# A decoder layer with product-key experts: the bf16 high half of the gated activations moves from VectorE to ScalarE, and U blocks are loaded one place earlier on SyncE's queue

## The chip, the cores and the metric

The kernel runs on one core of a Trainium2 chip. The metric is device time in microseconds (us), the median of several runs. Engines are named as the profile names them: PE (TensorE, matrix products; PEld is its weight load), DVE (VectorE), ACT (ScalarE), POOL (GpSimd) and SP (SyncE, which here only issues DMA transfers). A "q" behind a name (SPq) is the engine's sequencer, the part that waits for semaphores and issues DMAs.

## The reference

One decoder layer over 1024 tokens of width 1024: two kinds of attention, a layer norm, then PEER, a layer of 16384 single-neuron experts of which each token uses 16 per head, and a second layer norm. The change touches only the expert part:

```
u = expert_u[idx]
h = gelu(einsum('thkd,td->thk', u, xb), approximate=False)
w = (g * h).astype(xb.dtype)
return einsum('thk,thkd->td', w, expert_v[idx])
```

Here `idx` are the chosen experts and `g` their softmax weights. Inputs and results are float32.

## The kernel before

The kernel has three phases: attention, routing (query products, top-k, a table of gates in device memory) and the expert phase, in which all of the change lies. The expert phase treats the tokens in two ways at once.

Five of the eight tiles of 128 tokens are computed **densely**: every one of the 16384 experts is evaluated for all 640 tokens, and the gate, zero for the experts that were not chosen, picks out the result. The experts come in 128 blocks of 128. For a block b, `up` multiplies the U block with the tokens (`h_psum`), ACT applies Gelu into `act_out` (L1595), DVE multiplies by the gate (L1665), and `down` multiplies with the V block into `o_psum`. Because PE works on bf16 and the data are float32, every operand is split into a bf16 high half (a copy to bf16) and a bf16 low half (value minus high half), and three of the four products are summed. So for each block there are three splits: U (`u_split`: high half on ACT L1587, low half on DVE L1677), V (`v_split`: ACT L1604, DVE L1688) and the gated activations (`w_split`: high half on DVE L1667, low half on DVE L1669).

The other three tiles are **gathered**: POOL fetches, for each of their 128 tokens, the rows of U (first half of the phase) or V (second half) of the experts chosen, 512 KB at a time, by indirect DMA into a ring of six buffers (L1641). DVE consumes each fetch in one instruction, here called a pick (L1702 for U, L1706 for V). There are 6 picks for each block on average.

The blocks go in groups of four, 32 groups in all. PE's order in a group is: up, down of tile 0, up, down of tile 1, up, down of tile 2, up, down of tile 3, down of tile 4 (`up_and_down`). The downs of a group run while the ups of the next group are made. DVE's work for one block is called a **step** in this document, and its four steps in a group are steps 0 to 3. A step is `gate_and_split`, then the low half of U for block b+2, then the low half of V for block b, then picks and the addition of one finished `o_psum` tile into the accumulator (L1694). By the table `DOWN_TILES`, steps 0 to 2 have one addition and 4, 5 and 5 picks; step 3 has two additions and 10 picks. `o_psum` is double-buffered, so the down of a tile waits until DVE has added the tile two places before it.

ACT's order for a block is: Gelu of b, high half of V of b, high half of U of b+2 (`blocks_of`). SP's order is in `refill`: wait until U's split of block b is done, load U of b+2; wait until V's split of block b is done, load V of b+2; after every fourth block wait for `w_done` and load the gates of a later group (L1552, 1280 KB). The raw U and V blocks have two buffers each. All of these transfers are on SP's queue and are issued in that order; the fetches are on POOL's queue.

## Time and profile before

| | |
|---|---|
| median of 3 runs | 3163.55 us (3163.04 to 3173.81) |
| the profiled execution's own time | 3160.89 us |
| its span, first to last instruction | 3159.1 us |
| PE busy | 2749.3 us, 87% |
| DVE busy | 2502.0 us, 79% |
| ACT busy | 770.7 us, 24% |
| POOL busy | 1137.8 us, 36% |
| mean granted PE clock | 0.925 |

The busy shares are means over phases with different limits. The expert phase is the last 1.9 ms of the span, and there PE, DVE and the DMA engines are all nearly full, so what bounds it has to be read from single groups: where each engine sits idle, and what ended that idle time. The granted clock is given as a fraction of full speed (1.0 is 2.4 GHz, 0.5 is 1.2 GHz).

### The profile page before, as it was taken

Reading aid. Unit: us, or ns where it says so; the run is one execution under the profiler, and the core shown is the slowest. Engines: PE = TensorE matmul, PEld = TensorE weight load, DVE = VectorE, ACT = ScalarE, POOL = GpSimd, SP = SyncE. Lnnn points to the kernel's source line nnn. Section 1 sums busy time; section 2 is a strip of 40 time slices with the busy share of each in tenths; the row PEclk is TensorE's granted clock in tenths of the full one; section 3 lists DMA queues with packets and bytes.
Section 4 is the critical chain, followed back from the end, with each engine's and each line's share of the span. In section 5 each row is a group of like instructions: output and inputs, shape, how many; then the busy total and the mean of one; then the engine's idle time right before and its main releaser. Section 6 shows DMA issues by size and latency. Waiting matters only on the chain. (4 is left out here: it accounts for less than half of the span.)

```text
span 3159.1 us, 47167 instructions
## 1 busy us (share of the span) xinstructions
PE 2749.3 (87%) x17293; PEld 1762.0 (56%) x17459; DVE 2502.0 (79%) x4669; ACT 770.7 (24%) x1295; POOL 1137.8 (36%) x841
## 2 busy tenths in 40 slices
PE   8999999798967745599999999989999899999995
PEld 3666655458966644355555555555555555555552
DVE  3344545366999998589889898988989998989998
ACT  2333323211124446112121121211212112112120
POOL 2110000110010000355555555555555555555554
PEclk9999988799978865799999999999999999999998
DMA  3000020260002243899989999989899898999993
GB/s 144 21 14 15 14 74 14 100 234 21 2 27 107 107 167 164 312 329 321 315 316 321 323 324 329 321 299 334 307 316 317 313 321 304 314 313 317 327 315 142
DMA packets 262961, 685.26 MB, mean 217 GB/s; under 512 B 35625, under 2 KB 118185, under 8 KB 258353
## 3 DMA queue, kind: packets, MB, share of 16 engines
q0 software_dynamic: 110592, 402.70, 35.6%
q1 hardware_dynamic: 152240, 280.98, 25.5%
q8 instruction: 64, 1.05, 0.1%
q14 instruction: 65, 0.52, 0.1%
HBM read 624.89 MB, written 58.72 MB: 216 GB/s over the span
## 5 line engine op out<-in xcount | busy, mean ns | idle before, releaser
L1831 PE MATMUL o_psum<-v_split,w_split 128*128 128x512 bf16 x3713 | 866.1, 391 | 123.6 <-DVE wide L1694 111.8
L1813 PE MATMUL h_psum<-early 128*128 128x384 bf16 (+1 forms) x6144 | 860.5, 300 | 51.0 <-DVE early L1677 26.0
L1813 PEld LDWEIGHTS h_psum<-early 128*128 128x128 bf16 x6144 | 602.0, 98 | 310.6 <-issue 61.0
L1831 PEld LDWEIGHTS o_psum<-v_split,w_split 128*128 128x128 bf16 x3840 | 382.5, 100 | 587.4 <-DVE wide L1694 123.9
L1641 POOL DMA_INDIRECT early<-u_rows,pick_index x320 | 419.8, 1312 | 444.7 <-DVE dots L1702 324.4
L1641 POOL DMA_INDIRECT early<-v_blocks,pick_index x320 | 423.0, 1322 | 380.4 <-DVE wide L1706 308.3
L1706 DVE SCALAR_TENSOR_TENSOR wide<-early,dots,wide 128x1024 f32<-128x1024 f32 x320 | 400.0, 1280 | 61.2 <-DMA early<-v_blocks,pick_index 59.3
L1702 DVE CUSTOM_DVE_ANT_0 early<-early,wide 128x1024 f32<-128x1024 f32 x320 | 382.1, 1220 | 68.9 <-DMA early<-u_rows,pick_index 65.7
L1587 ACT ACTIVATE early<-early 128x1024 bf16<-128x1024 f32 x128 | 135.2, 1057 | 1101.2 <-DMA early<-u_blocks 1090.6
L1100 PE MATMUL r_t_psum<-rt_x_t,early 128*128 128x128 f32 (+1 forms) x1920 | 237.5, 286 | 0.0
L1100 PEld LDWEIGHTS r_t_psum<-rt_x_t,early 128*128 128x128 f32 x1920 | 232.3, 202 | 0.0
L1130 PE MATMUL g_psum<-rt_hot 128*128 128x128 bf16 x1280 | 119.3, 263 | 127.8 <-DVE rt_hot L1435 127.5
L1694 DVE SCALAR_TENSOR_TENSOR wide<-wide,o_psum 128x1024 f32<-128x1024 f32 x160 | 194.3, 1214 | 0.0
L1201 ACT ACTIVATE wide<-g_psum 128x512 f32<-128x512 f32 x160 | 157.2, 1087 | 150.4 <-PE g_psum L1130 150.4
L1595 ACT ACTIVATE act_out<-h_psum 128x384 f32<-128x384 f32 (+1 forms) x256 | 96.8, 430 | 372.5 <-PE h_psum L1813 364.9
L1677 DVE TENSOR_TENSOR early<-early 128x1024 bf16<-128x1024 f32 x128 | 155.9, 1219 | 35.3 <-ACT early L1587 22.1
L1130 PEld LDWEIGHTS g_psum<-rt_hot 128*128 128x128 bf16 x1280 | 102.6, 119 | 143.5 <-DVE rt_hot L1435 70.8
L1688 DVE TENSOR_TENSOR v_split<-early,v_split 128x1024 bf16<-128x1024 f32 x128 | 155.9, 1218 | 0.0
L1604 ACT ACTIVATE v_split<-early 128x1024 bf16<-128x1024 f32 x128 | 135.4, 1058 | 0.0
L559 DVE TENSOR_SCALAR att_o_rows<-a_o_psum,att_row_sum 128x64 f32<-128x64 f32 x64 | 18.2, 284 | 130.3 <-PE a_o_psum L348 129.8
L1665 DVE TENSOR_TENSOR act_out<-act_out,gate 128x640 f32<-128x640 f32 x128 | 105.9, 827 | 13.0 <-ACT act_out L1595 8.6
L1669 DVE TENSOR_TENSOR w_split<-act_out,w_split 128x640 bf16<-128x640 f32 x128 | 105.7, 826 | 4.4
(200 smaller groups left out, 3014.7 us busy)
## 6 DMA issues: line engine op xcount, KB each, us to landing
early<-u_blocks SPq DMA_DIRECT2D x128, 512.0 KB
early<-v_blocks SPq DMA_DIRECT2D x128, 512.0 KB
gates<-wide SPq DMA_DIRECT2D x20, 2048.0 KB, 6.4
gate<-gates SPq DMA_DIRECT2D x32, 1280.0 KB
early<-w_query SPq DMA_DIRECT2D x8, 1024.0 KB, 5.8
att_w_raw<-w_fox SPq DMA_DIRECT2D x4, 1536.0 KB, 7.0
early<-u_rows,pick_index POOLq DMA_INDIRECT x320
early<-v_blocks,pick_index POOLq DMA_INDIRECT x320
```

Source lines behind the costliest of these rows:

```text
L1100: mm = pe.matmul(t_psum[n % 2][:, j * P:(j + 1) * P], w_q[:, unit, c], x1_t[:, c, bass.ds(tile_of(t) * P, P)], start=(c == 0), stop=(c == ...
L1130: mm = pe.matmul(g_psum[four % 2][:, j % 4], hot[:, m % HOTS, 1, j // 2, :, j % 2], hot[:, m % HOTS, 2 + part, j // 2, :, j % 2], start=(p ...
L1201: act.activation(stage[:, k, :, token:token + 4].rearrange("p h t -> p t h"), g_psum[four][:, :, :], ACT.Copy).then_inc(g_copied, 1)
L1604: act.activation(v_split[:, p, q, 0], v_raw[:, j % 2], ACT.Copy).then_inc(v_hi_done, 1)
L1641: pool.indirect_dma_start(fetched[n % RING], None, source, bass.IndirectOffsetOnAxis(ap=pick_index[:, n % GATHERED, at:at + 1], axis=0)).t ...
L1677: dve.tensor_tensor(u_split[:, k, 1], u_raw[:, k].rearrange("p (c n) -> p c n", c=KD), u_split[:, k, 0], ALU.subtract).then_inc(u_lo_done, 1)
L1688: dve.tensor_tensor(v_split[:, p, q, 1], v_raw[:, q % 2], v_split[:, p, q, 0], ALU.subtract).then_inc(v_split_done, 1)
L1694: dve.scalar_tensor_tensor(row, row, scale, o_psum[(DENSE * p + t) % 2][:, :], ALU.mult, ALU.add).then_inc(o_added, 1)
L1702: dve.tensor_tensor_reduce(fetched[n % RING], fetched[n % RING], acc[:, tile], 1.0, 0.0, ALU.mult, ALU.add, dots[:, k, tile:tile + 1]).the ...
L1706: dve.scalar_tensor_tensor(acc[:, tile], fetched[n % RING], dots[:, k, tile:tile + 1], acc[:, tile], ALU.mult, ALU.add).then_inc(row_used, 1)
L1813: mm = pe.matmul(h_psum[k][:, half, 0:width * P], u_split[:, k, part, c], xs[:, first:first + width, xpart, c, :], start=(c == 0 and part ...
L1831: mm = pe.matmul(o_psum[(DENSE * p + t) % 2][:, half * 512:half * 512 + 512], w_split[:, p, q, part, t * P:(t + 1) * P], v_split[:, p, q, ...
```

## The change

There are two edits.

The high half of the gated activations is made by ACT (`split_w_hi`), behind the high half of U in ACT's order and ahead of the next block's Gelu. DVE keeps the product with the gate (`gate_block`) and the low half (`split_w_lo`), and the low half now stands behind the step's first picks, just ahead of its addition, instead of right behind the product.

SP loads a U block as soon as the U split of the block before it in the same buffer is done: in iteration b it loads U of b+4 ahead of the wait for V's split of b; before, it loaded U of b+2 there. Two loads ahead of the loop make up the difference.

```diff
                     for j in range(2 * GROUP):
                         b = 2 * GROUP * i + j
+                        if not (end and j >= 2 * GROUP - 4):
+                            sp.wait_ge(u_hi_done, b + 3)
+                            sp.wait_ge(u_lo_done, b + 3)
+                            load_u(b + 4, j % 2)
                         if not (end and j >= 2 * GROUP - 2):
-                            sp.wait_ge(u_hi_done, b + 1)
-                            sp.wait_ge(u_lo_done, b + 1)
-                            load_u(b + 2, j % 2)
                             sp.wait_ge(v_split_done, b + 1)
                             load_v(b + 2, j % 2)
...
+                def split_w_hi(b, j):
+                    act.wait_ge(gated, b + 1)
+                    act.activation(w_split[:, j // GROUP, j % GROUP, 0], act_out[:, j % 2], ACT.Copy
+                                   ).then_inc(w_hi_done, 1)
...
                             split_u_hi(b + 2, j % 2, GROUP * i + j // 2 + 2)
+                        split_w_hi(b, j)
...
                     dve.tensor_tensor(rows, rows, gate[:, p, :, q, :], ALU.mult).then_inc(gated, 1)
-                    dve.wait_ge(gated, b + 1)
-                    dve.tensor_copy(w_split[:, p, q, 0], act_out[:, k]).then_inc(w_hi_done, 1)
+
+                def split_w_lo(b, p, q):
                     dve.wait_ge(w_hi_done, b + 1)
-                    dve.tensor_tensor(w_split[:, p, q, 1], act_out[:, k], w_split[:, p, q, 0], ALU.subtract
+                    dve.tensor_tensor(w_split[:, p, q, 1], act_out[:, q % 2], w_split[:, p, q, 0], ALU.subtract
                                       ).then_inc(w_done, 1)
...
                                 take(i, kind, half * p + r)
+                            if t == DOWN_TILES[q][0]:
+                                split_w_lo(GROUP * g + q, p, q)
```

DVE's instructions of step 1 in the loop over the first half of the phase, before (L1665 is the product, L1667 and L1669 the high and low half of the activations, L1677 and L1688 the low halves of U and V, L1702 a pick, L1694 the addition):

```order
L1665 TENSOR_TENSOR act_out<-act_out,gate 128x640 [waits gelu_done]
L1667 CAST w_split<-act_out 128x640 [waits gated]
L1669 TENSOR_TENSOR w_split<-act_out,w_split 128x640 [waits w_hi_done]
L1674 REGISTER_ALU [waits u_in1]
L1677 TENSOR_TENSOR early<-early 128x1024 [waits h_done,u_hi_done]
L1688 TENSOR_TENSOR v_split<-early,v_split 128x1024 [waits v_hi_done,v_in1]
L1702 ISA early,dots<-early,wide 128x1024 [waits fetched_in4]
L1702 ISA dots 128x1
L1702 ISA fetched,dots<-fetched,wide 128x1024 [waits fetched_in5]
```

The same step after the change, where the lines are L1676 (product), L1688 and L1699 (U and V), L1713 (pick), L1680 (low half of the activations) and L1705 (addition):

```order
L1676 TENSOR_TENSOR act_out<-act_out,gate 128x640 [waits gelu_done]
L1685 REGISTER_ALU [waits u_in1]
L1688 TENSOR_TENSOR early<-early 128x1024 [waits h_done,u_hi_done]
L1699 TENSOR_TENSOR v_split<-early,v_split 128x1024 [waits v_hi_done,v_in1]
L1713 ISA early,dots<-early,wide 128x1024 [waits fetched_in4]
L1713 ISA dots 128x1
L1713 ISA fetched,dots<-fetched,wide 128x1024 [waits fetched_in5]
L1713 ISA dots 128x1
L1711 ISA
L1713 ISA early,dots<-early,wide 128x1024 [waits fetched_in0]
L1713 ISA dots 128x1
L1680 TENSOR_TENSOR w_split<-act_out,w_split 128x640 [waits w_hi_done]
```

The cast is gone, nothing that the next instruction needs stands right behind the product any more, and the low half has moved behind three picks (two in steps 0 and 3).

ACT's instructions for two blocks at the start of its loop, after the change (L1600 Gelu, L1609 high half of V, L1592 of U, L1613 of the gated activations; before, the rows are the same without L1613):

```order
L1600 ACTIVATE act_out<-h_psum 128x384 [waits w_done]
L1600 ACTIVATE act_out<-h_psum 128x256
L1609 ACTIVATE v_split<-early 128x1024 [waits o_done]
L1592 ACTIVATE early<-early 128x1024 [waits h_done,u_in0]
L1613 ACTIVATE w_split<-act_out 128x640 [waits gated]
L1596 REGISTER_ALU
L1600 ACTIVATE act_out<-h_psum 128x384 [waits w_done,h_done]
```

The next block's Gelu now stands behind an instruction that waits for DVE's product.

## Rows read from the trace of the kernel before

**Rows 1.** Windows: expert phase, groups, part of steps 1, 3; clock, DMA share last.

```profile
core 0: us, PE busy (x) PEld busy (x) DVE busy (x) ACT busy (x) POOL busy (x), PEclk, DMA share, GB/s
1295.76:3092.02 1796.26, 1667.16 (x9672) 965.13 (x9795) 1624.92 (x1950) 345.28 (x509) 988.77 (x756) 0.97 0.90 317
1920.13:1976.32 56.19, 55.12 (x326) 32.18 (x330) 50.98 (x76) 10.95 (x16) 32.71 (x25) 1.00 0.92 325
2722.76:2779.67 56.91, 51.91 (x301) 30.00 (x304) 51.86 (x50) 9.35 (x15) 31.43 (x25) 0.97 0.91 317
1930.23:1941.48 11.25, 11.20 (x70) 6.74 (x70) 11.18 (x17) 2.77 (x4) 6.66 (x5) 1.00 0.86 301
1952.73:1962.73 10.00, 9.95 (x65) 6.27 (x65) 9.93 (x15) 0.20 (x2) 5.81 (x4) 1.00 0.83 275
1962.73:1976.32 13.59, 13.54 (x81) 7.92 (x81) 8.65 (x16) 1.55 (x3) 8.60 (x7) 1.00 1.05 382
1966.00:1976.00 10.00, 9.95 (x65) 6.28 (x65) 6.17 (x10) 0.00 (x0) 5.71 (x6) 1.00 1.04 397
```

**Rows 2.** Waits in 1295.76:3092.02: us in total, times, longest.

```profile
ACT early L1587 <- DMA early<-u_blocks: 1090.6, 125, 20.4
PE o_psum L1831 <- DVE wide L1694: 92.8, 31, 5.5
DVE early L1702 <- DMA early<-u_rows,pick_index: 65.7, 33, 5.4
DVE wide L1706 <- DMA early<-v_blocks,pick_index: 59.3, 25, 5.9
DVE early L1677 <- ACT early L1587: 22.1, 6, 6.0
```

**Rows 3.** Timeline of step 1: start, length, instruction, idle before it and its releaser.

```profile
1926.21 6.68 PE L1813 MATMUL h_psum<-early 128*128 128x384 bf16 x48
...
1930.23 0.82 DVE L1665 TENSOR_TENSOR act_out<-act_out,gate 128x640 f32<-128x640 f32 x1
...
1931.08 0.49 DVE L1667 CAST w_split<-act_out 128x640 bf16<-128x640 f32 x1
1931.61 0.83 DVE L1669 TENSOR_TENSOR w_split<-act_out,w_split 128x640 bf16<-128x640 f32 x1
...
1932.35 1.22 DVE L1677 TENSOR_TENSOR early<-early 128x1024 bf16<-128x1024 f32 x1
...
1932.95 5.13 PE L1831 MATMUL o_psum<-v_split,w_split 128*128 128x512 bf16 x23
...
1934.62 1.22 DVE L1702 CUSTOM_DVE_ANT_0 early<-early,wide 128x1024 f32<-128x1024 f32 x1
```

**Rows 4.** Timeline of step 3 of the same group.

```profile
1952.73 0.82 DVE L1665 TENSOR_TENSOR act_out<-act_out,gate 128x640 f32<-128x640 f32 x1
...
1957.23 0.33 SPq L1478 DMA_DIRECT2D early<-v_blocks  x1
1957.78 0.56 SPq L1552 DMA_DIRECT2D gate<-gates  x1
...
1959.04 5.01 SPq L1478 DMA_DIRECT2D early<-u_blocks  x1
1959.12 1.17 POOL L1641 DMA_INDIRECT early<-u_rows,pick_index  x1 [3.38 <-DVE dots L1702]
...
1962.51 5.13 PE L1831 MATMUL o_psum<-v_split,w_split 128*128 128x512 bf16 x23
...
1968.62 1.23 DVE L1702 CUSTOM_DVE_ANT_0 early<-early,wide 128x1024 f32<-128x1024 f32 x1 [3.41 <-DMA early<-u_rows,pick_index]
```

**Rows 5.** Waits of SP's sequencer in 1295:3092.

```profile
SPq L1478 <- DVE v_split L1688: 1458.2, 126, 19.0
```

**Rows 6.** ACT's groups by shape in 1390:3110: busy us, mean ns.

```profile
L1604 ACT ACTIVATE v_split<-early 128x1024 bf16<-128x1024 f32 x120 | 126.9, 1058 | 0.0
...
L1595 ACT ACTIVATE act_out<-h_psum 128x384 f32<-128x384 f32 x120 | 58.0, 483 | 353.5 <-PE h_psum L1813 345.8 <-DVE w_split L1669 5.6 <-issue 1.8
```

More of the change, by code:

```diff
@@ L1571, in refill @@
                             load_gate(2 * i + 2 + j // GROUP, j // GROUP)
+                for b in range(2):
+                    sp.wait_ge(u_hi_done, b + 1)
+                    sp.wait_ge(u_lo_done, b + 1)
+                    load_u(b + 2, b)
                 with sp.Fori(0, last) as i:
@@ L1655, in _, with gate_block @@
                 dve.memset(eps[:, :], LN_EPS).then_inc(eps_set, 1)
-                def gate_and_split(b, g, p, q, n):
+                def gate_block(b, g, p, q, n):
                     k = q % 2
@@ L1727, in step @@
                     for q in range(GROUP):
-                        gate_and_split(GROUP * g + q, g, p, q, n)
+                        gate_block(GROUP * g + q, g, p, q, n)
                         split_u_lo(i, GROUP * g + q + 2, GROUP * p + q)
```

## The prediction

> **What bounds the kernel now.** Only the expert phase is touched, so I read that first, with the table of windows over the stretch from the first product with a gate to the last, and then over single groups of four blocks. In the 1796.26 us of the phase PE is busy 1667, DVE 1625 and the DMA share is 0.90 [rows 1]. The distance between the two ends is 127 steps, or 31.75 groups, so a group takes 56.6 us on average. The reader is to see that no engine is far from full, and that a busy share alone doesn't say which one sets the pace.
>
> The waits do. PE's largest wait is for DVE's additions: 92.8 us in 31 waits, one in each group [rows 2]. ACT waits 1090.6 us for U blocks, but ACT is busy only 345 us of the phase, and what it delays is small: DVE waits for ACT's high half of U in 6 places, 22.1 us together [rows 2]. DVE itself waits only for fetches, 65.7 + 59.3 us [rows 2]. So PE waits for DVE, and DVE either works or waits for a fetch: DVE with its fetches is the chain.
>
> Where in a group? In step 1 DVE is busy 11.18 of 11.25 us while the DMA share is 0.86 at 301 GB/s [rows 1]: the step is DVE's own work, and the transfers have room. In the steady group I read, DVE is busy 50.98 of 56.19 us [rows 1]; the idle 5.2 us lie in step 3, whose seventh pick waits 3.41 us for its fetch [rows 4]. In the first 10 us of step 3 the DMA share is 0.83 at 275 GB/s, and in ten later ones 1.04 at 397 [rows 1]. So steps 0 to 2 are bound by DVE, and the second part of step 3 by transfers.
>
> A comparison that the trace makes by itself: the group in the second half of the phase, with the same bytes, has 0.88 us more of DVE work (51.86 against 50.98) and is 0.72 longer (56.91 against 56.19) [rows 1]. A microsecond of DVE's work is worth nearly a microsecond.
>
> **Edit 1, the high half on ACT.** In step 1 the starts are: product 1930.23, cast 1931.08, low half 1931.61, low half of U 1932.35 [rows 3]. So the three cost 0.85 + 0.53 + 0.74 = 2.12 us. The low half, 0.83 us long and followed by an instruction that doesn't need it, costs 0.74; the product, 0.82 long, is now followed by such an instruction too, and I give it the same 0.74. After the change the two cost 1.48, so a step loses 0.64. If the product keeps its 0.85, the step still loses 0.53. Steps 0 to 2 are 96 of the 128: 96 x 0.64 = 61 us, at least 96 x 0.53 = 51.
>
> What hides the work that is moved: ACT's copy of 640 columns. The trace doesn't show it; it shows 1058 ns for 1024 columns and 483 ns for 384 [rows 6], which bound it, and on the line between them 640 columns come to 0.71 us. I take that. DVE asks for the result only after the low halves of U and V (1932.35 to 1934.62, 2.27 us) and two or three picks of 1.22 [rows 3], which is 4.7 us or more after the product. ACT is then not held by something else: its copy of U for b+2 stands ahead, and that block is now in place a step earlier. So the copy costs nothing; without its cover it would cost 0.71 on every step.
>
> The Trainium skill speaks against this move: in "ScalarE: Activation LUTs", Rules for kernel authors, simple elementwise work belongs on VectorE, which is there the faster engine per element. The rows agree that DVE is faster here (0.49 us for the cast against 0.71 estimated on ACT), and by the rule with the copy on the path the change would lose 0.18 us a step instead of gaining 0.53. It is not on the path as the rows stand.
>
> What waits behind the new wait: ACT's Gelu of b+1 is queued behind the copy, so it can't start before the product of b has ended, some 1.5 us into the step. PE's next use of that buffer is a whole block later, so nothing asks for it sooner. And the low half comes later: at 0.74 + 2.27 + 2.4 = 5.4 us into the step, done at 6.2, against 2.2 before. PE's first down of a group needs the fourth block's low half; it starts at 1962.51, which is 9.8 us after the start of step 3 at 1952.73 [rows 4]. The margin of 3.6 us covers a PE that runs up to that much further ahead. SP's load of gates, behind the same wait, is issued at about +6.2 instead of +5.05; it is for a later group.
>
> **Edit 2, U one place earlier.** SP's waits are nearly all for V's split, 1458.2 us in 126 [rows 5]: the U load, whose own condition was long met, stood behind it. In step 3 the loads were issued at +4.5 (V), +5.05 (gates) and +6.3 (U), and U's issue itself took 5.01 us behind the gates [rows 4]. After the change U goes out when its own low half is done, at 0.74 + 1.14 = +1.9, V at about +3.0, gates at +6.2. The same bytes move, but U and V fill the first ten microseconds of step 3, where the DMA engines have room, and U no longer competes with the fetches behind the gates. A U block is 0.52 MB, 1.3 us at the 397 GB/s of the later stretch [rows 1]. That is the most by which the last fetch of the step can come earlier from this. The seventh pick's fetch (issued at 1959.12, +6.4) is used at 1968.62, and in front of it are V and the gates; after the change also U. So the seventh pick hardly moves against the step's start and only what follows it is quicker. I take 0.8 us a group, 32 x 0.8 = 26 us. Bounds: below, the seventh pick comes a U block later, -1.3 a group; above, all of DVE's waiting goes until PE is the limit. PE's work in a group is 4 x 6.68 + 5 x 5.13 = 52.4 us [rows 3, 4], so a group can gain 56.6 - 52.4 = 4.2 at most, of which 1.9 is in steps 0 to 2, and 2.3 is left for step 3.
>
> The DMA page of the Trainium skill ("DMA: Bandwidth & Descriptors", Bandwidth) puts the limit between device memory and one core at about 358 GB/s. The row shows 397 over ten microseconds, so the trace doesn't agree for this one core. By the page's figure step 3, which moves 10 us x 275 GB/s and then 13.6 us x 382 GB/s [rows 1], some 7.9 MB, could not go under 22 us, an estimate that would leave 1.5 us of gain there.
>
> The six waits for U's high half (22.1 us) should mostly go, since U is there a step earlier; the first, 6.0, follows the first loads of the phase and stays. Of the other 16 I take 12.
>
> Against this I set 10 us, 0.3 a group, for places where PE and DVE, now both near their own limits, hold each other up.
>
> **The sum.** 61 + 26 + 12 - 10 = 89 us. The profiled execution took 3160.9, so 3071.9; the median of the runs lies 2.7 above the profiled one, which gives 3074. The parts of the span before and behind the phase don't change.
>
> **Rivals.**
> 1. Step 3 gives nothing: the last fetch lands at the same distance from the step's start, because the same bytes pass in it. For it: the gates' transfer still stands in front of the seventh fetch. Against it: the room in the first ten microseconds. The sum without the 26: 3100.
> 2. PE becomes the bound: the fetches no longer hold DVE, and a group takes PE's 52.4 plus 0.5 for joints. (56.6 - 52.9) x 32 = 118: 3045. For it: PE has only 92.8 us of that wait, and its granted clock is 0.97 over the phase, a mean of stretches at 2.4 GHz and a few at 1.2, against 1.00 in the steady group [rows 1]; some of that would come back. Against it: step 3's transfers.
> 3. Transfers take it all back: share 0.90 in the phase already, so DVE's saved time turns into waiting for fetches. 3160. Against it: the comparison of the two halves of the phase, and 0.86 in step 1.
> 4. Slower: in step 3 U, V and gates (0.52 + 0.52 + 1.31 = 2.36 MB) stand together on SP's queue in front of the seventh fetch, and hold all fetches behind it. At the 275 GB/s of that stretch they take 8.6 us. If the seventh pick is used later than now by more than the 1.9 us that steps 0 to 2 save, the group gets longer; with 2.7 later it is 0.8 x 32 = 26 us slower, 3189. It decides itself at +17.8 us into step 3, against +15.9 now. Against it: fetches and SP's loads are on different queues and share the engines, and the gates are issued later than now.
>
> **Chances.** The forecast 0.45 (its own range 3055 to 3092), rival 1 0.22, rival 2 0.19, rival 3 0.07, rival 4 0.07. Range for 8 in 10: from 3038, near rival 2's PE limit, to 3116, which takes in rival 1 with the lower price of 0.53 a step. About 0.5%, 16 us, is what a measurement can tell from no change. Faster 0.87, same 0.06, slower 0.07.
>
> **What would show it.** Steps 1 and 2 at 10.6 us instead of 11.25, with DVE still full in them; step 3 near 22.5 instead of 23.6 with the seventh pick's wait still there; the U load issued 1.9 us into a step and ACT's wait for it nearly gone, ACT waiting for the product instead; the low half never waiting for ACT's copy, about 0.7 us; PE's wait for the additions down from 3 us a group to about 1. I am wrong if step 3 grows by as much as the others shrink (transfers), if the low half waits for ACT, or if PE waits for `w_done` at the first down of a group.

## The result and the profile after

| | before | after |
|---|---|---|
| median | 3166.12 us (3163.04 to 3173.81, 4 runs) | 3024.33 us (3020.01 to 3029.14, 4 runs) |
| profiled execution, span | 3160.89, 3159.1 | 3029.14, 3027.3 |
| expert phase, first to last product | 1796.26 us | 1664.88 us |
| sum of steps 0 / 1 / 2 / 3 over the groups | 353.0 / 363.8 / 362.2 / 717.3 | 318.9 / 351.7 / 343.8 / 650.4 |

The kernel is faster: the ratio is 0.9554, interval 0.9539 to 0.957. I had forecast 3074 with a range of 3038 to 3116, so the direction was right and the size wrong: the gain is 142 us, not 89, and the time lies below the range. The 128 products have 127 distances between them: 32 each for steps 0 to 2, and 31 for step 3. The step sums in the last line are worked out from their start times in the trace. Steps 0 to 2 gave 64.6 us together and step 3 gave 66.9. All of the gain lies in the expert phase (131.4 of the 131.8 us between the two profiled executions). The other 10 us of the 142 are spread between executions: the median lies 5 us above the profiled execution before, and 5 below it after.

The windows of the kernel after: the phase, one group, its step 1, and its step 3 in two parts, to be read against [rows 1]. The group read takes 53.88 us by DVE's products, longer than the mean of 52.4 (1664.88 / 31.75), and its step 3 takes 22.8 us against a mean of 21.0.

```profile
core 0: us, PE busy (x) PEld busy (x) DVE busy (x) ACT busy (x) POOL busy (x), PEclk, DMA share, GB/s
1295.27:2960.15 1664.88, 1629.12 (x9662) 957.76 (x9785) 1555.72 (x1822) 427.38 (x636) 1118.71 (x756) 0.99 0.95 342
1868.68:1922.56 53.88, 53.67 (x323) 31.79 (x326) 48.93 (x72) 13.34 (x20) 33.80 (x26) 1.00 0.97 352
1878.13:1888.73 10.60, 10.55 (x67) 6.54 (x67) 10.60 (x16) 2.29 (x5) 7.18 (x5) 1.00 1.02 398
1899.79:1909.79 10.00, 10.00 (x49) 4.70 (x48) 8.99 (x14) 2.42 (x3) 5.62 (x4) 1.00 0.84 284
1909.79:1922.56 12.77, 12.72 (x81) 7.82 (x80) 9.20 (x16) 2.65 (x4) 8.54 (x8) 1.00 1.03 368
```

DVE's work in the phase fell by 69.2 us (1624.92 to 1555.72), which is the 128 casts and little else. The phase fell by 131.4, so DVE's idle time fell by the other 62.2. PE is now idle for 35.8 us of the phase, against 129.1 before, and the same bytes pass at 342 GB/s instead of 317. PE is also busy for 38.0 us less (1667.16 to 1629.12) with the same products. Before, the granted clock stood at its lower level, 1.2 GHz, for 92.2 us of the phase in 19 stretches; after, for 20.5 us in 5. At half the clock half of a stretch is lost, which makes 35.9 us of the difference. Before, 13 of the 19 stretches begin within 1.3 us of the end of a stand of PE of 3.0 to 4.9 us, as in this row, where the 24 products take 7.04 us instead of 5.34, with a granted clock of 0.53 from 2351.00 to 2354.40:

```profile
2350.39 7.04 PE L1831 MATMUL o_psum<-v_split,w_split 128*128 128x512 bf16 x24 [4.49 <-DVE wide L1694]
```

In step 1 DVE has no idle time, and the step takes 10.60 us instead of 11.25.

The waits of the kernel after in the phase that answer to those of [rows 2], and ACT's new one:

```profile
ACT w_split L1613 <- DVE act_out L1676: 540.8, 103, 18.3
...
DVE wide L1717 <- DMA early<-v_blocks,pick_index: 38.6, 53, 2.4
DVE early L1713 <- DMA early<-u_rows,pick_index: 32.6, 34, 2.7
...
PE o_psum L1844 <- DVE wide L1705: 15.2, 12, 4.2
DVE early L1688 <- ACT early L1592: 13.8, 10, 8.3
...
ACT early L1592 <- DMA early<-u_blocks: 7.1, 1, 7.1
```

Four things are to be read there. PE's wait for the additions fell from 92.8 us in 31 waits to 15.2 in 12. DVE's waits for fetches fell in these two rows from 125.0 us to 71.2, and the longest from 5.9 to 2.7. ACT's wait for U blocks (1090.6 us) is gone but for the first. And ACT's largest wait, for the product, has no one behind it: the list has no wait of DVE's low half for ACT's copy at all. One of the prediction's signs of being wrong, PE waiting for `w_done`, shows once, 5.9 us at PE's first down, and not in the groups behind it.

The same group's step 1, of which [rows 3] has the one before (product, low half of U, ACT's copy, low half of V, the two loads, the late low half, the addition, the next product):

```profile
1878.13 0.82 DVE L1676 TENSOR_TENSOR act_out<-act_out,gate 128x640 f32<-128x640 f32 x1
1878.87 1.22 DVE L1688 TENSOR_TENSOR early<-early 128x1024 bf16<-128x1024 f32 x1
1878.98 0.74 ACT L1613 ACTIVATE w_split<-act_out 128x640 bf16<-128x640 f32 x1 [0.80 <-DVE act_out L1676]
...
1880.36 0.34 SPq L1478 DMA_DIRECT2D early<-u_blocks  x1
...
1884.58 0.82 DVE L1680 TENSOR_TENSOR w_split<-act_out,w_split 128x640 bf16<-128x640 f32 x1
...
1885.32 1.21 DVE L1705 SCALAR_TENSOR_TENSOR wide<-wide,o_psum 128x1024 f32<-128x1024 f32 x1
...
1888.73 0.82 DVE L1676 TENSOR_TENSOR act_out<-act_out,gate 128x640 f32<-128x640 f32 x1
...
1889.92 1.23 DVE L1688 TENSOR_TENSOR early<-early 128x1024 bf16<-128x1024 f32 x1 [0.36 <-ACT early L1592]
```

Product and low half take 0.74 us each from start to next start, as assumed; ACT's copy is done at 1879.72, and its reader starts 4.86 us later. The last row, in step 2, has a small new wait: ACT's high half of U comes 0.36 us late, behind the Gelu that PE's up released. In step 3 the same wait is 1.01 us. This is how PE's pace now reaches DVE.

Step 3 of that group, against [rows 4]: the loads, the seventh pick, and the waits behind it.

```profile
1899.79 0.82 DVE L1676 TENSOR_TENSOR act_out<-act_out,gate 128x640 f32<-128x640 f32 x1
...
1903.06 0.33 SPq L1478 DMA_DIRECT2D early<-u_blocks  x1
...
1907.19 0.56 SPq L1552 DMA_DIRECT2D gate<-gates  x1
...
1912.84 1.23 DVE L1713 CUSTOM_DVE_ANT_0 early<-early,wide 128x1024 f32<-128x1024 f32 x1
...
1915.61 1.23 DVE L1713 CUSTOM_DVE_ANT_0 early<-early,wide 128x1024 f32<-128x1024 f32 x1 [0.41 <-DMA early<-u_rows,pick_index]
...
1918.10 1.23 DVE L1713 CUSTOM_DVE_ANT_0 early<-early,wide 128x1024 f32<-128x1024 f32 x1 [1.25 <-DMA early<-u_rows,pick_index]
...
1920.27 1.23 DVE L1713 CUSTOM_DVE_ANT_0 fetched<-fetched,wide 128x1024 f32<-128x1024 f32 x1 [0.94 <-DMA fetched<-u_rows,pick_index]
```

The seventh pick starts 13.05 us into the step, where it started at 15.89 before, and the profile shows no wait for its fetch; before it waited 3.41. The waits at the three last picks have grown, from 0.67 us together to 2.60. The 31 steps 3 of each trace, taken together, say the same with other sizes, and show what each edit does to the pick:

| kernel | seventh pick starts at | it waits | the three last picks wait |
|---|---|---|---|
| before | +16.38 us | 3.65 us | 0.55 us |
| U ahead of the gates, one place | +15.76 | 2.99 | 0.51 |
| U early, alone (edit 2) | +15.06 | 2.34 | 0.43 |
| after | +13.13 | 0.33 | 1.57 |
| after, gates earlier | +14.48 | 0.94 | 0.28 |

(Means, worked out from the start times of DVE's picks; the kernels between before and after are those of the next section.) The pick moved by 3.25 us, 1.32 of them with edit 2 alone. The step became only 2.2 us shorter, because part of the wait came back behind the pick. My prediction had both parts wrong: the pick moves, and what follows it does not become quicker.

### The profile page after: what moved, and what is told of

It is laid out like the page before. It is cut to its first block, busy times and chain, and to the rows that moved or that the text cites. A ratio compares the mean times of both kernels' runs of the same rounds, so it can differ in the third digit from the quotient of the medians.

```text
span 3027.3 us, 47212 instructions
## 1 busy us (share of the span) xinstructions
PE 2715.5 (90%) x17293; PEld 1756.0 (58%) x17459; DVE 2432.0 (80%) x4541; ACT 853.5 (28%) x1423; POOL 1268.7 (42%) x841
## 4 chain that ended last, share of the span: by engine, by line
PE 23%; issue 12%; DMA 10%; DVE 9%; POOL 2%; SPq 1%; ACT 0%; DVEq 0%; POOLq 0%; ACTq 0%
PE h_psum L1826 12%; PE o_psum L1844 11%; DMA early<-v_blocks,pick_index 6%; DMA fetched<-v_blocks,pick_index 3%; DVE wide L1717 2%; POOL early L1652 2%; DVE early L1713 1%; DVE early L1688 1%; DVE v_split L1699 1%; DVE wide L1705 1%; DMA fetched<-u_rows,pick_index 1%; DVE act_out L1676 1%; SPq L1552 1%; POOL fetched L1652 1%; DVE w_split L1680 1%
## 5 line engine op out<-in xcount | busy, mean ns | idle before, releaser
L1844 PE MATMUL o_psum<-v_split,w_split 128*128 128x512 bf16 x3713 | 832.0, 382 | 46.2 <-DVE wide L1705 33.6
L1844 PEld LDWEIGHTS o_psum<-v_split,w_split 128*128 128x128 bf16 x3840 | 375.9, 98 | 482.5 <-DVE wide L1705 40.1
L1652 POOL DMA_INDIRECT early<-v_blocks,pick_index x320 | 491.4, 1536 | 229.0 <-DVE wide L1717 146.3
L1652 POOL DMA_INDIRECT early<-u_rows,pick_index x320 | 441.5, 1380 | 332.4 <-DVE dots L1713 212.0
L1713 DVE CUSTOM_DVE_ANT_0 early<-early,wide 128x1024 f32<-128x1024 f32 x320 | 382.6, 1220 | 34.5 <-DMA early<-u_rows,pick_index 32.6
L1613 ACT ACTIVATE w_split<-act_out 128x640 bf16<-128x640 f32 x128 | 94.3, 736 | 637.5 <-DVE act_out L1676 544.7
L1600 ACT ACTIVATE act_out<-h_psum 128x384 f32<-128x384 f32 (+1 forms) x256 | 97.4, 432 | 610.2 <-PE h_psum L1826 553.8
L1705 DVE SCALAR_TENSOR_TENSOR wide<-wide,o_psum 128x1024 f32<-128x1024 f32 x160 | 194.0, 1212 | 0.0
L1688 DVE TENSOR_TENSOR early<-early 128x1024 bf16<-128x1024 f32 x128 | 155.8, 1218 | 24.3 <-ACT early L1592 13.8
L1699 DVE TENSOR_TENSOR v_split<-early,v_split 128x1024 bf16<-128x1024 f32 x128 | 155.7, 1217 | 0.0
L1592 ACT ACTIVATE early<-early 128x1024 bf16<-128x1024 f32 x128 | 135.1, 1056 | 17.9 <-PEq L1070 10.8
L1609 ACT ACTIVATE v_split<-early 128x1024 bf16<-128x1024 f32 x128 | 135.4, 1058 | 1.4 <-DMA early<-v_blocks 1.4
L1676 DVE TENSOR_TENSOR act_out<-act_out,gate 128x640 f32<-128x640 f32 x128 | 105.0, 820 | 14.1 <-ACT act_out L1600 9.0
```

The source lines that it names most:

```text
L1609: act.activation(v_split[:, p, q, 0], v_raw[:, j % 2], ACT.Copy).then_inc(v_hi_done, 1)
L1652: pool.indirect_dma_start(fetched[n % RING], None, source, bass.IndirectOffsetOnAxis(ap=pick_index[:, n % GATHERED, at:at + 1], axis=0)).t ...
L1688: dve.tensor_tensor(u_split[:, k, 1], u_raw[:, k].rearrange("p (c n) -> p c n", c=KD), u_split[:, k, 0], ALU.subtract).then_inc(u_lo_done, 1)
L1699: dve.tensor_tensor(v_split[:, p, q, 1], v_raw[:, q % 2], v_split[:, p, q, 0], ALU.subtract).then_inc(v_split_done, 1)
L1705: dve.scalar_tensor_tensor(row, row, scale, o_psum[(DENSE * p + t) % 2][:, :], ALU.mult, ALU.add).then_inc(o_added, 1)
L1713: dve.tensor_tensor_reduce(fetched[n % RING], fetched[n % RING], acc[:, tile], 1.0, 0.0, ALU.mult, ALU.add, dots[:, k, tile:tile + 1]).the ...
```

## The experiments

Each was timed beside the kernel before on the same chip; those runs of before had medians from 3164.02 to 3170.45. "Phase" is the distance between first and last product of the profiled execution, and the steps are sums over the groups, worked out as above.

| kernel | median us | ratio (interval) | phase | steps 0 / 1 / 2 / 3 |
|---|---|---|---|---|
| before | 3166.12 | | 1796.3 | 353 / 364 / 362 / 717 |
| U early, alone (edit 2) | 3104.57 | 0.9812 (0.9779 to 0.9846) | 1735.0 | 338 / 363 / 362 / 672 |
| U ahead of the gates, one place | 3125.32 | 0.986 (0.9827 to 0.9892) | 1761.7 | 339 / 364 / 362 / 697 |
| ACT high half, alone (edit 1) | 3250.25 | 1.0266 (1.0228 to 1.0305) | 1882.9 | 495 / 345 / 356 / 686 |
| the same, gates earlier | 3179.4 | 1.0025 (0.9995 to 1.0056) | 1835.0 | 435 / 353 / 356 / 691 |
| the same, U ahead of the gates | 3092.92 | 0.9768 (0.9742 to 0.9794) | 1732.3 | 319 / 376 / 352 / 685 |
| after | 3024.33 | 0.9554 (0.9539 to 0.957) | 1664.9 | 319 / 352 / 344 / 650 |
| after, gates earlier | 3033.75 | 0.9588 (0.9556 to 0.9621) | 1664.5 | 319 / 354 / 344 / 648 |
| after, cast on DVE | 3076.87 | 0.9726 (0.9698 to 0.9753) | 1708.8 | 335 / 359 / 358 / 657 |
| after, low half at once | 3136.39 | 0.9894 (0.9869 to 0.9918) | 1776.3 | 348 / 371 / 370 / 688 |
| after, half picks | 2996.39 | 0.9457 (0.9435 to 0.9478) | 1635.8 | 261 / 366 / 359 / 650 |
| before, gates in step 1 | 3332.29 | 1.052 (1.0482 to 1.0559) | 1966.0 | 333 / 376 / 648 / 608 |
| U early, gates in step 1 | 3025.08 | 0.956 (0.9529 to 0.959) | 1662.3 | 334 / 363 / 367 / 599 |
| after, gates in step 1 | 3000.48 | 0.9472 (0.945 to 0.9494) | 1637.1 | 319 / 356 / 358 / 605 |

### The two edits apart

**U early, alone.** The kernel before with edit 2.

```diff
+                        if not (end and j >= 2 * GROUP - 4):
+                            sp.wait_ge(u_hi_done, b + 3)
+                            sp.wait_ge(u_lo_done, b + 3)
+                            load_u(b + 4, j % 2)
                         if not (end and j >= 2 * GROUP - 2):
-                            sp.wait_ge(u_hi_done, b + 1)
-                            sp.wait_ge(u_lo_done, b + 1)
-                            load_u(b + 2, j % 2)
                             sp.wait_ge(v_split_done, b + 1)
```

> The kernel before with edit 2 alone: SP issues U of b+4 ahead of the wait for V's split; the high half stays on DVE. Theory A (step 3 got shorter because U no longer stands behind the gates on SP's queue): step 3 falls from 23.2 us to about 21.5, the six waits for U's high half go, and the time is near 3166 - 32 x 1.7 - 16 = 3096. Theory B (it got shorter because the gates' transfer is issued behind the seventh pick's fetch instead of ahead of it): here the gates are still issued ahead of that fetch, so the seventh pick's wait stays 3 us or more, step 3 loses 0.5 at most, and the time is near 3166 - 16 - 16 = 3134.

**ACT high half, alone.** The kernel before with edit 1.

```diff
+                def split_w_hi(b, j):
+                    act.wait_ge(gated, b + 1)
+                    act.activation(w_split[:, j // GROUP, j % GROUP, 0], act_out[:, j % 2], ACT.Copy
+                                   ).then_inc(w_hi_done, 1)
...
-                    dve.wait_ge(gated, b + 1)
-                    dve.tensor_copy(w_split[:, p, q, 0], act_out[:, k]).then_inc(w_hi_done, 1)
...
+                            if t == DOWN_TILES[q][0]:
+                                split_w_lo(GROUP * g + q, p, q)
```

> The change with edit 1 alone: high half on ACT, low half behind the first picks, SP's order as before. The gates, which wait for the low half, are issued about 7 us into step 3, behind the seventh pick's fetch. Theory A (U's place made step 3 shorter): step 3 stays at 23, steps 0 to 2 lose 0.64 each, the waits for U stay: 3166 - 61 = 3105. Theory B (the gates' place): step 3 falls to about 21.2 us although U is issued late, and the time is near 3166 - 61 - 60 = 3045, U's hiccups keeping it above the change's 3024.

Edit 2 alone saves 61 us, 45 of them in step 3, where I had given it 26, and 15.5 in step 0. The first theory fits: step 3 takes 672.2 / 31 = 21.7 us where it gave 21.5, the time is 9 us above its 3096, and the seventh pick's wait is under the 3 us of the second theory. Edit 1 alone costs 85 us, which neither theory had (3105 and 3045). Together they save 142, so they are not a sum of two parts: the second makes the first possible. The loss is not in ACT or DVE's work (step 1 is down by 18 us). It is in step 0, whose sum rose from 353 to 495. This is the timeline around the joint of steps 3 and 0, in the kernel with edit 1 alone:

```profile
1933.98 0.56 SPq L1552 DMA_DIRECT2D gate<-gates  x1
...
1934.78 11.72 SPq L1478 DMA_DIRECT2D early<-u_blocks  x1
...
1948.40 0.82 DVE L1671 TENSOR_TENSOR act_out<-act_out,gate 128x640 f32<-128x640 f32 x1
...
1955.51 1.06 ACT L1587 ACTIVATE early<-early 128x1024 bf16<-128x1024 f32 x1 [15.00 <-DMA early<-u_blocks]
...
1956.60 1.22 DVE L1683 TENSOR_TENSOR early<-early 128x1024 bf16<-128x1024 f32 x1 [7.38 <-ACT early L1587]
```

The late low half holds back the gates on SP's queue (they wait for `w_done`), the issue of U behind them takes 11.72 us where the same issue behind a V block takes 0.33, U lands only after step 0 has begun, ACT's high half is late, and DVE stands for 7.38 us. The kernel before escapes it narrowly at the same place, here in the step 0 that follows [rows 4]:

```profile
1977.00 1.06 ACT L1587 ACTIVATE early<-early 128x1024 bf16<-128x1024 f32 x1 [12.72 <-DMA early<-u_blocks]
...
1978.45 1.22 DVE L1677 TENSOR_TENSOR early<-early 128x1024 bf16<-128x1024 f32 x1
```

ACT's copy ends at 1978.06 and DVE asks for it 0.39 us later. Edit 1 lets DVE ask 1.4 us earlier in the step. ACT's start also tells when the block had landed, since it waited for it: before, 16.4 us (median of 30, from 13.5 to 23.3) after the start of an issue right behind the gates, and 5.7 us (4.0 to 7.4) behind a V block. The block is 10.7 us late, although the gates' 1.31 MB are worth 3.3 us at 397 GB/s. Sometimes the kernel before waits as well: "DVE early L1677 <- ACT early L1587: 22.1, 6, 6.0" in [rows 2] is the same wait. With edit 1 alone it has grown to

```profile
DVE early L1683 <- ACT early L1587: 185.3, 51, 9.5
```

### Where U's early load pays

**U ahead of the gates, in one place of four.** The kernel before, with one load moved.

```diff
-                            sp.wait_ge(u_hi_done, b + 1)
-                            sp.wait_ge(u_lo_done, b + 1)
-                            load_u(b + 2, j % 2)
+                            if j % GROUP:
+                                sp.wait_ge(u_hi_done, b + 1)
+                                sp.wait_ge(u_lo_done, b + 1)
+                                load_u(b + 2, j % 2)
                             sp.wait_ge(v_split_done, b + 1)
                             load_v(b + 2, j % 2)
+                        if j % GROUP == GROUP - 1 and not (end and j == 2 * GROUP - 1):
+                            sp.wait_ge(u_hi_done, b + 2)
+                            sp.wait_ge(u_lo_done, b + 2)
+                            load_u(b + 3, (j + 1) % 2)
```

> The kernel before with one move: in the one place of four where a group's gates are fetched (step 3), the load of U is issued ahead of the gates instead of behind them. In the other steps U keeps its place behind the wait for V's split, and ACT's work is that of before. Theory 1: all that U's move (edit 2) gives in step 3 comes from this one place, where U's issue stood behind the gates' transfer. Then step 3 takes 21.0 to 21.8 us instead of 22.4, which is some 40 of edit 2's 61 us, and the time is 3115 to 3130 us. Theory 2: what counts is U's earlier start in every step, which takes it off the fetches that follow. Then this move gives little, step 3 stays above 22.2 us, and the time is 3145 to 3165 us.

The time, 3125.3, fell in the band of the first theory, but by its parts neither theory holds whole. The phase lost 34.5 us of the 61.3 that edit 2 gives: 14.5 of step 0's 15.5, and 20.6 of step 3's 45. A step 3 takes 696.7 / 31 = 22.5 us; the first theory wanted 21.0 to 21.8. So a good half of edit 2's gain is this one place. The rest goes with the other difference between the two kernels, U's earlier start in each step (3.6 us into it instead of 5.1). The step 3 read in each trace shows the same order: the seventh pick waited 3.41 us before [rows 4], and in this kernel and with edit 2 alone, one row each:

```profile
1951.65 1.22 DVE L1710 CUSTOM_DVE_ANT_0 early<-early,wide 128x1024 f32<-128x1024 f32 x1 [3.14 <-DMA early<-u_rows,pick_index]
```

```profile
1944.98 1.23 DVE L1707 CUSTOM_DVE_ANT_0 early<-early,wide 128x1024 f32<-128x1024 f32 x1 [1.97 <-DMA early<-u_rows,pick_index]
```

Why this last half is so large is not settled. The same bytes pass in the step, and a U block is 0.52 MB, 1.3 us; yet step 3 with edit 2 alone is 45 / 31 = 1.5 us shorter. What shrinks is DVE's idle time in step 3, by 44.7 us (142.0 to 97.3, over 31 steps). The trace doesn't say which DMA engine carried which packet, so I can't show whether one engine lagged behind the others.

**ACT high half with the gates earlier, and with U ahead of the gates.** Edit 1 alone, and in the one kernel the gates wait for the product instead of the low half,

```diff
                         if j % GROUP == GROUP - 1 and not end:
-                            sp.wait_ge(w_done, b + 1)
+                            sp.wait_ge(gated, b + 1)
```

while in the other U is moved ahead of the gates in one place, with the lines of the diff above.

> Edit 1 alone again, but the gates' load waits for the product instead of for the low half, so that it is issued about 3 us earlier in step 3 and U's load of the next step stands less far behind. Theory C (edit 1 alone is slower because the low half, now late, holds back the gates on SP's queue and U behind the gates, so that U comes after step 0 has asked for it): step 0 falls from 15.7 us to 10 to 11, DVE's 185 us of waits for ACT's high half of U shrink under 60, and the time is near 3110. Theory D (it is slower because ACT's copy for the activations stands in front of its other work): step 0 stays at 15 us and the time near 3250.

> Edit 1 alone, with SP's order as before except at one place in four: the U load that followed the gates on SP's queue is issued ahead of them; the other three stay behind V's split. Theory C (edit 1 alone was 85 us slower because U stood behind the gates' transfer while DVE asked for it 1.4 us earlier in the step and step 3 was shorter): step 0 falls from 15.7 us to about 10, and with steps 1 and 2 at 10.6 to 11 and step 3 near 21 the time is near 3040. If U's later place in the other three steps matters as well: steps 1 and 2 above 11.2, or DVE's waits for the high half of U above 40 us in all, and 3080 to 3120.

The gates' earlier issue brought 71 of the 85 us back. Step 0 still costs 435 us, or 13.6 a step, and the waits for ACT's high half are 136.8 us, so the result lies between theories C and D, and the delay of the gates is only a part of the cause. In the second kernel U's place took step 0 to 319, the value of the kernel after, and made a gain of 73 us of a loss of 85. So the loss of edit 1 is the place of U behind the gates, and the delay of the gates makes it longer. But this kernel still stands 69 us above the kernel after, in the band of the expectation's second case. Its steps 1 and 3 are longer (376 against 352, 685 against 650), and ACT's high half of U is late in 38 places, 57.1 us together:

```profile
ACT early L1595 <- DMA early<-u_blocks: 653.7, 101, 11.0
...
DVE early L1691 <- ACT early L1595: 57.1, 38, 8.4
```

A U block that is loaded just before it is needed has no reserve once steps are shorter. Edit 2's load runs one block further ahead in every step, and that is what the shorter steps need.

**After, gates earlier.** The kernel after with the same exchange of `w_done` for `gated`: the gates go out 3.7 us into step 3 instead of 6.4 (medians).

> The changed kernel with the gates' load waiting for the product (the last reader of the gates) instead of for the low half, so that it is issued right behind V's load, at about 3.5 us into step 3 and ahead of the seventh pick's fetch. Theory B: the seventh pick waits 2 to 3 us again, step 3 grows from 20.7 to about 22.5, and the time is near 3024 + 32 x 1.5 = 3072. Theory A: no change, 3024 within 8 us.

The length of step 3 did not change: 648 us against 650, in a phase of 1664.5 against 1664.9. The median is 9 us higher, just outside the 8 of theory A, but the intervals of the two ratios overlap. So the theory that step 3 became short because the gates now stand behind the seventh fetch falls. The place of the gates does decide which pick waits, though: with the gates earlier the seventh pick starts 1.35 us later and the three last picks wait 1.29 us less (the table of the last section). In the kernel after, moving the gates by 2.7 us moves the wait and does not remove it.

### Edit 1, taken apart

**After, cast on DVE.** The high half goes back to DVE, right behind the product; the low half stays late.

```diff
-                        split_w_hi(b, j)
...
                     dve.tensor_tensor(rows, rows, gate[:, p, :, q, :], ALU.mult).then_inc(gated, 1)
+                    dve.wait_ge(gated, b + 1)
+                    dve.tensor_copy(w_split[:, p, q, 0], act_out[:, k]).then_inc(w_hi_done, 1)
```

> The changed kernel with the high half back on DVE, right behind the product; the low half stays late and U early. It prices ACT's copy alone against the cast. If DVE bounds steps 0 to 2: each step is 0.63 us longer, and the time rises by what PE's limit of 51.8 us a group doesn't swallow: 3024 + 96 x 0.64 = 3085, to 3105 with step 3. It also shows whether the low half's late place, without the cast's move, does anything: if so the time differs by over 15 us from the 3104.6 of edit 2 alone.

**After, low half at once.** ACT makes the high half, and DVE's low half stands right behind the product again, so that ACT's copy is on DVE's path.

```diff
                         gate_block(GROUP * g + q, g, p, q, n)
+                        split_w_lo(GROUP * g + q, p, q)
                         split_u_lo(i, GROUP * g + q + 2, GROUP * p + q)
...
-                            if t == DOWN_TILES[q][0]:
-                                split_w_lo(GROUP * g + q, p, q)
```

> The changed kernel with the low half of the activations put back right behind the product, the high half still on ACT, so that ACT's 0.74 us copy lies on DVE's path in every step. If the cover of the first picks is what makes the copy free: each step costs some 0.75 to 0.9 us more, 1.0 where ACT is still at U's high half; in the half bound by DVE all of it shows, in the other part of it, so 3024 + 128 x 0.6 = 3100. If the cover is worth nothing (PE sets the time anyway): within 15 us of 3024.

From edit 2 alone (3104.6) to the cast on DVE with a late low half (3076.9) is 28 us, and from there to the kernel after (3024.3) is 53. So the two halves of edit 1 give 28 for the order and 53 for the engine, once U has its reserve; by the profiled phases it is 26 and 44. Of the 26, step 3 has 15.4, nearly all of it idle time of DVE (97.3 to 82.2 us). With the low half out of the way, DVE's first picks and SP's loads of U and V stand 0.9 us earlier in the step, and the gates 1.8 us later; which of these does it, no run shows. The time lies 8 us below the 3085 of the expectation.

With the copy on the path, the kernel is 112 us slower than after (3136.4, where I expected 3100), and also 32 us slower than edit 2 alone, which has the same order and the cast on DVE. The wait is there by name:

```profile
DVE w_split L1680 <- ACT w_split L1613: 102.2, 117, 9.2
```

That is 0.25 us a block (32 / 128) in the very comparison for which I had worked out 0.18. The Trainium skill's rule ("ScalarE: Activation LUTs", Rules for kernel authors: simple elementwise work goes to VectorE) holds here where the copy is waited for, and is turned round where 4.86 us of other work cover it.

### What limits the kernel now

**After, half picks.** Each pick works on 512 of its 1024 columns. This leaves out half of the sums of the gathered tiles, and all transfers stay.

```diff
-                        dve.tensor_tensor_reduce(fetched[n % RING], fetched[n % RING], acc[:, tile], 1.0, 0.0,
+                        dve.tensor_tensor_reduce(fetched[n % RING][:, 0:HALF], fetched[n % RING][:, 0:HALF],
+                                                 acc[:, tile, 0:HALF], 1.0, 0.0,
```

> The changed kernel with DVE's picks on the first 512 of the 1024 columns of each fetched row; all transfers stay. It leaves out half of the gathered dot products and sums. DVE loses about 0.53 us on each of 768 picks, 13 us in a group of 52. If PE is the bound of the changed kernel: PE's start-to-start 4 x 6.74 + 5 x 4.96 = 51.8 us a group remains and the time falls only from 3024 to about 3005. If DVE with its fetches still is the bound: it falls by 8 us a group or more, below 2800.

DVE's work in the phase falls by 392 us, and the time by 28. The starts of PE's ups (L1829) and downs (L1847) in a group show why:

```profile
1912.18 6.68 PE L1829 MATMUL h_psum<-early 128*128 128x384 bf16 x48
...
1918.70 5.34 PE L1847 MATMUL o_psum<-v_split,w_split 128*128 128x512 bf16 x24
...
1923.88 6.68 PE L1829 MATMUL h_psum<-early 128*128 128x384 bf16 x48
```

An up takes 6.52 us from start to next start and a down 5.18, so a group cannot be under 4 x 6.52 + 5 x 5.18 = 52.0 us at this clock. Taken from the start of every fourth up in each trace, 29 of 31 groups take 52.0 us in the kernel with half picks, all but the first two. In the kernel after it is 18 of 31, and in the kernel before none. So PE sets the pace of most groups of the kernel after; but for the first two, the others lie in the half that fetches V and take 52.4 to 58.1 us. The mean over the phase, 1635.8 / 31.75 = 51.5 us with half picks against 1664.9 / 31.75 = 52.4 in the kernel after, can lie under the floor of a full group because the first group's ups have no downs between them. The 28 us between the two kernels are what DVE with its fetches still costs.

**Gates in step 1.** The gates are loaded in step 1 instead of step 3, in three kernels: the one before, the one with edit 2 alone, and the one after.

```diff
-                        if j % GROUP == GROUP - 1 and not end:
-                            sp.wait_ge(w_done, b + 1)
-                            load_gate(2 * i + 2 + j // GROUP, j // GROUP)
+                        if j == 1:
+                            sp.wait_ge(w_done, b)
+                            load_gate(2 * i + 1, 1)
+                        if j == GROUP + 1 and not end:
+                            sp.wait_ge(w_done, b)
+                            load_gate(2 * i + 2, 0)
```

> The kernel before with one thing moved: the gates of a later group are loaded in step 1 of a group instead of step 3, one group later, so 1.31 MB leave step 3 and go where the DMA engines have room. Nothing else of the change is in it. Theory B (the gates' transfer ahead of the seventh fetch sets step 3): step 3 falls from 23.2 to about 20 us, bounded by DVE's own 18.2 there, steps 1 keep their 11.25, and the time is near 3166 - 32 x 2.7 = 3080. Theory A (U's place): step 3 stays above 22.5 and the time above 3140.

> Edit 2 alone with the gates in step 1, no edit 1. In the kernel before, the gates in step 1 cost 167 us. If that was U standing behind the gates with no step in hand, early U removes the cost: step 2 stays near 11.3 us, step 3 falls under 21 us as DVE's own 18.2 plus small waits allows, and the time is near 3104.6 - 31 x 1.5 = 3058. If V behind the gates was part of the cost, step 2 shows it, 12 us or more, and the time is above 3105.

> The changed kernel with the gates loaded in step 1 instead of step 3, the move that cost 167 us in the kernel before. If that cost came from U, which was needed within the step, it is gone here, since U now has a step in hand; V, which follows in the same queue and has no such reserve, could take its place. With U's reserve enough: step 3 shorter where DVE with its fetches is the bound, PE's 51.8 us a group the limit, 3005 to 3025. If V takes its place: step 2 grows by 5 us and more, 3150 or above.

The same move costs 167 us in the kernel before and gains 80 with edit 2 alone and 24 in the kernel after. No expectation had the 167 us (3080, or above 3140 with a long step 3), 3025 is 33 us better than the 3058 forecast for edit 2 alone, and 3000 is just under the range of 3005 to 3025 for the kernel after. It does what it is meant to do in all three: step 3 falls from 717 to 608, from 672 to 599 and from 650 to 605. But in the kernel before it puts U's issue behind the gates in step 1, and step 2 then stands for U: 648 us instead of 362. The trace of that kernel, and its wait:

```profile
1942.20 0.57 SPq L1552 DMA_DIRECT2D gate<-gates  x1
...
1943.01 7.25 SPq L1478 DMA_DIRECT2D early<-u_blocks  x1
...
1959.20 1.06 ACT L1589 ACTIVATE early<-early 128x1024 bf16<-128x1024 f32 x1 [15.77 <-DMA early<-u_blocks]
...
1960.29 1.22 DVE L1679 TENSOR_TENSOR early<-early 128x1024 bf16<-128x1024 f32 x1 [9.69 <-ACT early L1589]
```

```profile
DVE early L1679 <- ACT early L1589: 294.1, 40, 12.1
```

In the kernel after the slow issue is still there, and no one waits for it, because the block is for a step later:

```profile
1925.28 0.57 SPq L1552 DMA_DIRECT2D gate<-gates  x1
...
1934.90 3.33 SPq L1478 DMA_DIRECT2D early<-u_blocks  x1
```

The kernel after with its gates in step 1 is the fastest full version, 3000.48 us (2999.33 to 3002.37). PE's wait for the additions is one of 1.1 us there, and the phase is 1.4 us above that of the kernel with half picks: PE sets the pace, with 29 of 31 groups at 52.0 us. It also tells what edit 1 is worth when PE is nearly the bound: with U early and the gates in step 1, it adds 25 us (3025.1 to 3000.5), not 80.

```profile
PE o_psum L1846 <- DVE wide L1707: 1.1, 1, 1.1
```

## Why the prediction was wrong in size

**The step that failed: "the seventh pick hardly moves against the step's start and only what follows it is quicker. I take 0.8 us a group."** In the group read it moved from +15.89 to +13.05, in the mean from +16.38 to +13.13, and with edit 2 alone, which is what this step of the prediction was about, to +15.06. Step 3 lost 45.1 us with edit 2 alone, 1.5 us a group instead of 0.8. I had reckoned by bytes, the 1.3 us of one U block, in a step whose trace had a 5.01 us issue standing behind the gates [rows 4]. I wrote that row down and priced nothing from it. About half of the effect is that place (20.6 of 45 us); the other half goes with U's earlier start elsewhere, whose size I can't derive. Both edits together take 66.9 / 31 = 2.2 us from step 3, close to the 2.3 that I had named as the upper bound, but I had no reason for that size.

**The gap, term by term.** Against the profiled executions the gain is 131.8 us, and I had 89. Step 3 gave 19 more than forecast from edit 2 and 22 more from edit 1, no loss shows for which I had set 10 us aside ("hold each other up"), and steps 0 to 2 gave 8 less. The 10 us that are left to the 142 are the spread between executions.

**Edit 1 in step 3: taken as nothing, is 21.8 us.** I counted 96 steps because the second part of step 3 was bound by transfers. With edit 2 in place step 3 goes from 672.2 to 650.4 when edit 1 is added, 0.7 us a group: 13.9 us less of DVE's work and 7.9 less of its idle time. The fetches are themselves released by picks (POOL's issue at 1959.12 in [rows 4] waits for DVE's dots), so earlier picks also issue them earlier. That last reason is argued from the timeline; the kernel with the cast on DVE fits it, since it has 15.4 of the 21.8 us with the first picks 0.9 us earlier, but its loads of U and V go out earlier too.

**Edit 1 in steps 0 to 2: 61 us forecast, 48.4 measured.** With the waits for U I had 73, and the two edits together gave 64.6, but edit 2 alone has 16.2 of these, so edit 1 gave 48.4, under the 51 that I had called the least. The start-to-start times (0.74 and 0.74), the copy on ACT (0.71 estimated, measured below) and its cover held. DVE's own work in these steps fell by 54 us, 0.56 a step, and 6 us came back as new waits. Steps 1 and 2 of the group read are 10.60 and 11.06 us instead of 11.25. The second of them holds the new wait of 0.36 us. The copy's row:

```profile
L1613 ACT ACTIVATE w_split<-act_out 128x640 bf16<-128x640 f32 x128 | 94.3, 736 | 637.5 <-DVE act_out L1676 544.7
```

**The waits for U's high half: 12 of 16 us expected to go, 10.6 went.** With edit 2 alone all 16 went, and only the first, 5.9 us, stays. In the kernel after the first is 8.3 us of the 13.8; the other nine are 5.5, where five were 16.1. What I didn't see is that these six waits were the visible end of a mechanism: edit 1 alone makes 185.3 us of them. The prediction called that edit safe by itself ("ACT is then not held by something else: its copy of U for b+2 ... is now in place a step earlier") and leaned on edit 2 for it without asking what edit 1 does without. It was right about the pair.

**Rival 2, PE becomes the bound.** This is what happened in most groups; I gave it 0.19 and 3045 us. Its mechanism is shown three ways: 18 of 31 groups take the 52.0 us of PE's floor, PE's wait for the additions is 15.2 us, and half picks give only 28 us more. It missed its own time because I put the floor at 52.4 + 0.5. The 52.4 was added up from the lengths in the rows (6.68 and 5.13) and not from start to next start, which gives 52.0, and the 0.5 for joints does not show. The granted clock of the phase went from 0.97 to 0.99, as the rival said it would.

**Rival 1** (step 3 gives nothing) and **rival 3** (transfers take it back) are refuted: step 3 gave half of the phase's gain, and the rate of transfers rose from 317 to 342 GB/s with the demand. **Rival 4** (U, V and gates queue in front of the seventh fetch) is refuted by the seventh pick, which is at +13.13 in the mean, and at +14.48 even with the gates earlier, where the rival needed +17.8.

The limit of about 358 GB/s in the Trainium skill ("DMA: Bandwidth & Descriptors", Bandwidth) doesn't bind over a step here: step 1 moved 398 GB/s for 10.6 us. The same section says that with both cores of a memory domain streaming each gets about 358 GB/s, and it lists 425 GB/s for a 16 MB transfer on one core whose neighbour is idle, which is nearer to this kernel on one core and which I left out. Step 3 doesn't settle it. It takes 21.0 us on average (650.4 / 31) where the estimate from 358 GB/s gave 22, but in the group read it moved 7.5 MB (10.00 us at 284 GB/s and 12.77 at 368) and not 7.9, in 22.8 us.

## What to carry to other kernels

A load that stands behind a large transfer on one issuing queue is late by more than the bytes say (here 10.7 us behind 1.31 MB, which are worth 3.3 us at 397 GB/s): look in the timeline for an issue that takes microseconds instead of 0.33, and ask how many steps before its use the block was loaded. Two edits may each look like a separate saving and be worth -85 and +61 us alone and +142 together; before shortening a chain, give the loads that feed it a reserve. When PE waits 93 us for another engine and is busy for 93% of the stretch, work out PE's own floor from start-to-start times and give it a good chance of being the new end. A wait that has gone from one instruction may stand at the next ones: measure the whole step.

## What the runs showed of the hardware

The issue of a U block on SP's queue took 0.33 us behind a V block, and 4.20 to 12.87 us (median of 30: 5.29) right behind the gates' transfer of 1280 KB in the kernel before. From that issue to ACT's start on the block were 16.4 us (median) instead of 5.7. Issued in the next step instead, the block still took 3.02 us to issue (median) in the kernel after with the gates in step 1. The DMA engines of this core moved 398 GB/s over 10.6 us and 342 over 1.66 ms. ACT's copy of 128x640 from float32 to bf16 takes 0.736 us, DVE's cast of it 0.49. DVE's product of 128x640 takes 0.85 us to the next start where the next instruction waits for it, and 0.74 where it doesn't. An up of 48 products takes 6.52 us and a down of 24 takes 5.18 at the 2.4 GHz level. After PE had stood for 4.49 us, the granted clock was 0.53 over the next 3.4 us and the down took 7.04.
